# Routing of the last tiles and the closing stage rearranged in a decoder layer on one Trainium2 core

## What is computed

```python
        out = mix @ w_out[l]
        x = x + gate_m * rmsnorm(out, g_post_mix[l])

        h = rmsnorm(x, g_pre_ffn[l]) * (1.0 + scale_f) + shift_f
        y = hier_moe(h, w_router_g[l], b_router_g[l], w_router_e[l], b_router_e[l],
                     w_e_gate[l], w_e_up[l], w_e_down[l])
        x = x + gate_f * rmsnorm(y, g_post_ffn[l])
```

## Time and profile before

| | us |
|---|---|
| median of 3 runs | 769.46 |
| lowest and highest | 768.12 to 769.5 |
| the profiled execution | 773.03 |
| its span, first to last instruction | 771.4 |
| PE busy | 688.9 (89%) |
| VectorE (DVE) busy | 413.4 (54%) |
| ScalarE (ACT) busy | 291.5 (38%) |
| GpSimd (POOL) busy | 119.1 (15%) |
| moved by DMA | 179.27 MB, mean 232 GB/s |

### The profile page before, as it was taken

The page is one execution under the profiler, slowest core; times in us unless marked ns, Lnnn a source line. Parts: engine busy times, 40 slices in busy tenths (PEclk is TensorE's granted clock), DMA queues, the critical chain, the costliest instruction groups (busy, mean ns, idle before and its releaser), DMA issues.

```text
span 771.4 us, 9644 instructions
## 1 busy us (share of the span) xinstructions
PE 688.9 (89%) x3419; PEld 436.3 (57%) x3419; DVE 413.4 (54%) x876; ACT 291.5 (38%) x526; POOL 119.1 (15%) x143
## 2 busy tenths in 40 slices
PE   1899989999998989999999999989799979788873
PEld 0447757666676767777787788764333323233321
DVE  2376967998888877554423836645342211211118
ACT  5141336454586659442224333442221211211223
POOL 3056772320001101000000001010122211111100
...
GB/s 338 380 295 402 253 207 1 119 96 15 110 54 56 2 110 1 68 42 110 110 154 157 28 381 100 326 411 391 423 419 420 419 419 420 420 420 412 407 295 109
DMA packets 50270, 179.27 MB, mean 232 GB/s; under 512 B 9593, under 2 KB 13796, under 8 KB 36398
## 3 DMA queue, kind: packets, MB, share of 16 engines
...
...
## 4 chain that ended last, share of the span: by engine, by line
PE 43%; DVE 22%; DMA 7%; issue 7%; SPq 5%; ACT 4%; DVEq 0%; POOL 0%; ACTq 0%; POOLq 0%
PE psA L485 8%; PE psA L487 7%; PE psA L486 7%; PE psS L898 6%; PE psA L927 5%; SPq L1105 4%; DVE mk_mem L1856 4%; PE psG L898 4%; DVE m L1855 3%; DMA arena<-in_w_e_up_dram 3%; DVE arena_r L1804 2%; DMA y_dram<-sig_mem,tables 2%; DVE mk_mem L1895 1%; DVE qs_mem L1875 1%; DVE qs_mem L2023 1%
## 5 line engine op out<-in xcount | busy, mean ns | idle before, releaser
L485 PE MATMUL psA<-arena_r 128*128 128x512 f32 x320 | 129.6, 405 | 0.6 <-PE psA L487 0.6
L487 PE MATMUL psA<-arena_r 128*128 128x512 f32 x320 | 125.4, 392 | 0.0
L486 PE MATMUL psA<-arena_r 128*128 128x512 f32 x320 | 125.2, 391 | 0.0
L1804 DVE TENSOR_TENSOR arena_r<-arena,arena_r 128x1024 fp32r<-128x1024 f32 (+1 forms) x37 | 61.5, 1686 | 32.2 <-ACT arena_r L1322 31.1
L898 PE MATMUL psS<-arena,kv 128*64 128x512 f32 x224 | 62.9, 646 | 12.1 <-issue 9.7
L485 PEld LDWEIGHTS psA<-arena_r 128*128 128x128 f32 x320 | 60.7, 190 | 21.3 <-issue 9.5
L487 PEld LDWEIGHTS psA<-arena_r 128*128 128x128 f32 x320 | 60.4, 189 | 13.2
L486 PEld LDWEIGHTS psA<-arena_r 128*128 128x128 f32 x320 | 60.7, 190 | 11.8 <-issue 0.2
L898 PE MATMUL psG<-arena,kv 128*64 128x512 f32 x208 | 58.2, 611 | 5.0 <-issue 5.0
L1322 ACT CAST arena_r<-arena 128x1024 fp32r<-128x1024 f32 (+1 forms) x34 | 49.9, 1499 | 15.6 <-DMA arena<-in_w_in_dram 10.0
L2314 DVE TENSOR_TENSOR sig_mem<-sig_mem,psS 128x256 f32<-128x256 f32 x8 | 4.9, 613 | 81.1 <-ACT sig_mem L1642 81.1
...
## 6 DMA issues: line engine op xcount, KB each, us to landing
...
```

The source lines that it names most:

```text
L485: nc.tensor.matmul(acc, lhs[0], rhs[0], start=start, stop=False)
L486: nc.tensor.matmul(acc, lhs[0], rhs[1], start=False, stop=False)
L487: return nc.tensor.matmul(acc, lhs[1], rhs[0], start=False, stop=stop)
L1804: V.tensor_tensor(lo[:, part], src[:, part], hi[:, part], ALU.subtract).then_inc(lo_ready, 4 if q is None else 1)
```

## The change

At the routing of the last tiles: the squares of tile 3 are summed in halves with the copies of its transposes between; tile 2's rows are scaled and stored after tile 3's root; GpSimd makes the members, first_hot of tile 2 and the pair columns of tiles 2 and 3; PE runs slots(0), slots(1) and half of first_rows(0) ahead of tile 3's transposes, which go to banks S0 and A0; ranks(2) and position(2) come before route(3) on VectorE. The product of gates moves from there to after the gather of pair 1, its copy to pair 1. The third set of weights is issued in two parts, gate weights after k = 3 of the last output half, up weights at its end. In the closing stage all tiles go through the banks in order, and VectorE weighs tiles 0 and 1. At the layer's start one semaphore that nobody waits for is replaced by VectorE's own. The core of the diff:

```diff
         hi_n, lo_n = cnt[:, 5, 0:2 * TT], cnt[:, 6, 0:2 * TT]
         rowid = sb("rowid", [P, 2, TT, 2])
-        diag_e = kv[:, 1024:2048]
...
+                    if (tt, n, k) == (TT - 1, 1, 3):
+                        last.then_inc(ring_out, 1)
                 last.then_inc(full, 1)
-                if (tt, n) == (TT - 1, 1):
-                    pe.wait_ge(full, bank[where[("out", tt, 1)]].at[("out", tt, 1)] + 1)
-                    pe.sem_inc(ring_out, 1)
...
             def slots(tt):
...
-                pe.wait_ge(pos_ready, tt + 1)
+                if tt < 2:
+                    pe.wait_ge(pos_ready, tt + 1)
+                else:
+                    pe.wait_ge(pool_choice, columns[tt])
+                    if tt == 3:
+                        pe.wait_ge(pos_ready, 3)
+                    else:
+                        pe.wait_ge(dve_choice, lo2)
...
-            def first_rows(tt):
-
-                pe.wait_ge(hot_ready, tt + 1)
-                for half in range(2):
+            def first_rows(tt, halves=(0, 1)):
+
+                if tt == 2:
+                    pe.wait_ge(pool_choice, hot2)
+                else:
+                    pe.wait_ge(hot_ready, min(tt, 2) + 1)
+                for half in halves:
...
             router(2)
-            pe.wait_ge(spread_rows, 2)
-            gate_rows(diag_e, "gf", ("A0",))
-            x1_turn(3)
-            g = take("A1", ("gf", 1))
-            nc.tensor.matmul(g[:, :], ones[:, :], diag_e[:, 512:1024], start=True, stop=True).then_inc(bank["A1"].full, 1)
-            router(3)
             slots(0)
             slots(1)
-            first_rows(0)
+            first_rows(0, (0,))
+            x1_turn(3, ("S0", "A0"))
+            router(3)
+            ranks(2)
+            first_rows(0, (1,))
             first_rows(1)
-            ranks(2)
+            first_rows(2, (0,))
             ranks(3)
+            first_rows(2, (1,))
             slots(2)
-            first_rows(2)
             slots(3)
             first_rows(3)
+            gf_turn = [bank[f"A{n}"].turn(("gf", n)) for n in range(2)]
...
+            def ffn_gate_rows():
+
+                pe.wait_ge(spread_rows, 2)
+                for n in range(2):
+                    pe.wait_ge(bank[f"A{n}"].free, gf_turn[n])
+                    nc.tensor.matmul(ps[f"A{n}"][:, :], ones[:, :], diag_e[:, n * 512:(n + 1) * 512], start=True, stop=True).then_inc(bank[f"A{n}"].full, 1)
...
                 if j < NPAIR - 1:
                     turn_rows(j + 1, (j + 1) % 2, j // 2)
+                if j == 0:
+                    ffn_gate_rows()
...
-                    last = nc.tensor.matmul(ps[name][:, :], last_hot[:, tt, :], yb[:, 1, 512 * half:512 * (half + 1)], start=True, stop=(tt == 0))
-                if tt == 0:
-                    last.then_inc(sum_full, 1)
+                    nc.tensor.matmul(ps[name][:, :], last_hot[:, tt, :], yb[:, 1, 512 * half:512 * (half + 1)], start=True, stop=False)
...
             pe.wait_ge(yb_ready, NPAIR)
-            for tt in range(3):
+            for tt in range(TT):
                 last_part(tt)
-            other_part(1)
-            last_part(3)
-            other_part(2)
-            other_part(3)
+                other_part(tt)
...
+            def third_gate_up(n):
+                for q in range(2):
+                    src = (weg_v, weu_v)[n]
+                    sp.dma_start(gu_sets[2][q][:, 2048 * n:2048 * (n + 1)], src[4 + q]).then_inc(we_in[2], 16)
+
             sp.wait_ge(ring_out, len(items))
-            gate_up(2, 0, 4)
-            gate_up(2, 1, 5)
+            third_gate_up(0)
             down(1, 0, 2)
+            filled(sp, ("out", TT - 1, 1))
+            third_gate_up(1)
             down(1, 1, 3)
             sp.wait_ge(x1_ready, 2 * TT)
-            sp.wait_ge(xss_ready, TT)
+            sp.wait_ge(xss_ready, TT + 1)
...
-            pool.tensor_tensor(diag_e.rearrange("p (k n) -> p k n", k=KD), ident[:, :].unsqueeze(1).broadcast_to([P, KD, P]),
-                               gatev[:, 1, :].unsqueeze(2).broadcast_to([P, KD, P]), ALU.mult).then_inc(spread_rows, 1)
+            def members(tt):
+
+                pool.wait_ge(dve_choice, signed[tt])
+                step(pool.tensor_tensor(first_in[:, tt, :], e12[:, :, tt, 0], e12[:, :, tt, 1], ALU.subtract))
+                pool.tensor_tensor(first_in[:, tt, :], first_in[:, tt, :], st[:, 60 + tt:61 + tt].broadcast_to([P, 2]), ALU.mult).then_inc(pool_choice, 1)
...
+            def pair_columns(tt):
+
+                odd = e12[:, :, tt, :].rearrange("p w (n a) -> p w n a", a=2)
+                step(pool.tensor_tensor(pool_pair, odd[:, :, :, 0], odd[:, :, :, 1], ALU.subtract))
+                for w in range(2):
+                    ins = pool.tensor_tensor(hi_hot[:, tt, w, :, :], pool_pair[:, w, :].unsqueeze(1).broadcast_to([P, 2, NPAIR]),
+                                             rowid[:, w, tt, :].unsqueeze(2).broadcast_to([P, 2, NPAIR]), ALU.mult)
+                    if w == 0:
+                        step(ins)
+                    else:
+                        ins.then_inc(pool_choice, 1)
+                pool.wait_ge(pool_choice, columns[tt])
...
+            members(2)
+            pool.wait_ge(dve_choice, lo2)
+            step(pool.tensor_tensor(first_hot[:, 2, :], lo_hot[2][:, 0, :], first_in[:, 2, 0:1].broadcast_to([P, P]), ALU.mult))
+            step(pool.tensor_tensor(causal0[:, :], lo_hot[2][:, 1, :], first_in[:, 2, 1:2].broadcast_to([P, P]), ALU.mult))
+            pool.tensor_tensor(first_hot[:, 2, :], first_hot[:, 2, :], causal0[:, :], ALU.add).then_inc(pool_choice, 1)
+            pool.wait_ge(pool_choice, hot2)
+            pair_columns(2)
+            members(3)
+            pair_columns(3)
...
                     gather(src_i[:, j:j + 1], j % 2)
+                if j == 1:
+                    pool.tensor_tensor(diag_e.rearrange("p (k n) -> p k n", k=KD), ident[:, :].unsqueeze(1).broadcast_to([P, KD, P]),
+                                       gatev[:, 1, :].unsqueeze(2).broadcast_to([P, KD, P]), ALU.mult).then_inc(spread_rows, 1)
...
+            def last_half_squares(half):
+
+                act.wait_ge(x1_ready, 2 * TT - 1 + half)
+                nc.scalar.activation(scratch[:, 512 * half:512 * (half + 1)], x1(TT - 1)[:, 512 * half:512 * (half + 1)], ACT.Square,
+                                     accum_out=m8[:, 0:1] if half else st[:, 33:34]).then_inc(xss_ready, 1)
+
+            last_half_squares(0)
+            turned(3)
+            last_half_squares(1)
+            x1_root(3)
             store_rows(2)
-            x1_part(3)
             store_rows(3)
...
-                if j == 0:
+                if j == 1:
                     gate_copy()
...
-                if tt == 0:
-                    act.wait_ge(sum_ready, 1)
-                    nc.scalar.activation(scratch2, yc[:, tt, 0, :], ACT.Square, accum_out=st[:, tt:tt + 1]).then_inc(fms_ready, 1)
-                    return
...
             nc.scalar.activation(st[:, 44:45], st[:, 34:35], ACT.Sqrt)
-            first_choice(0)
-            first_choice(1)
-            square(0)
-            first_choice(2)
-            rooted(0)
-            first_choice(3)
-            for tt in range(1, TT):
+            for tt in range(TT):
                 square(tt)
+                if tt < 2:
+                    first_choice(tt + 2)
                 rooted(tt)
...
+            def mean_x1(tt):
                 dve.wait_ge(xss_ready, tt + 1)
+                if tt == TT - 1:
+                    dve.wait_ge(xss_ready, tt + 2)
+                    step(V.tensor_tensor(st[:, 33:34], st[:, 33:34], m8[:, 0:1], ALU.add))
                 rsqrt_in(st[:, 34:35], st[:, 33:34], D).then_inc(xms_ready, 1)
+
+            def scale_x1(tt):
                 dve.wait_ge(xsq_ready, tt + 1)
                 step(V.reciprocal(st[:, 60 + tt:61 + tt], st[:, 35:36]))
                 dve.sem_inc(xr_ready, 1)
 
+            def root_x1(tt):
+                mean_x1(tt)
+                scale_x1(tt)
...
-                dve.wait_ge(pos_ready, tt + 1)
+                dve.wait_ge(pos_ready, min(tt, 2) + 1)
+                if tt == TT - 1:
+                    dve.wait_ge(pool_choice, taken[3])
...
+                if tt >= 2:
+                    if tt == 2:
+                        mean_x1(3)
+                    V.tensor_tensor(e12[:, :, tt, :], e12[:, :, tt, :], sgn.unsqueeze(1).broadcast_to([P, 2, NE]), ALU.mult).then_inc(dve_choice, 1)
+                    dve.wait_ge(dve_choice, signed[tt])
+                    return
...
             route(2)
-            root_x1(3)
+            position(2)
+            scale_x1(3)
             route(3)
-            first_member(2)
-            first_member(3)
-            position(2)
-            first_slots(2)
             position(3)
             first_slots(3)
...
-                dve.wait_ge(fw_ready, tt + 1)
+                if tt < 2:
```

(41 more changed lines are left out.)

31 lines of the change are left out of this document (21 added, 10 removed).

## The result

| | before | after |
|---|---|---|
| median of 16 runs | 768.31 | 771.86 |
| lowest and highest | 765.71 to 770.73 | 770.13 to 773.91 |
| the profiled execution | 773.03 | 770.62 |
| its span | 771.4 | 769.1 |

The account below looks back on a forecast made before the run. The weights' DMA stream was taken to bound the kernel up to about 733 us, VectorE the tail; 1.2 us from stream holes plus 2.0 from the tail, 3.2 off the median 769.46, made 766.3 us, range 764.2 to 769.6.

Parts of the forecast that it names:

- product 0's end at 517.2: First expert pair's gate and up product: ends 2.4 us sooner, at 517.2 instead of 519.57; the set behind it issued then.
- the gather goes at 516.0: Gather of pair 1's rows on GpSimd: issued at 516.0, 2.9 us later than 513.07.
- I take 3.0: Time pair 1's gather takes: 3.0 us, between bounds of 2.6 (idle queue) and 7.82 (full queue), landing at 519.0.
- The queue ran dry: DMA queue ahead of the set behind product 0: all queued weights end near 517 us.
- the start of tile 3's routing: Tile 3's routing on VectorE: starts 0.4 us later than 502.26, waiting for position(2) and ranks(2).
- the squares in halves: Tile 3's squares in halves: copies come forward only by what the work put ahead of them takes, so no gain.
- The last store: Row stores on ScalarE: last issued at 506.0, not 504.13, queued behind the other, landing near 515.1.
- Product 1: Pair 1's gate and up product: runs 7.09 us as before, ending at 529.1 against 529.28.
- The stream: Expert weights' DMA stream: holes sum to 2.3 us instead of 3.5, so 1.2 us less.
- The third set's 2.07: Third weight set, issued at about 491 instead of 494.61: its stream hole of 2.07 us closes.
- The tail: Closing stage on VectorE: ends at 766.5 instead of 768.74, taken as 2.0 us less, between 1.0 and 3.0.
- The rival: Pair 1's gather takes 6.5 us, TensorE's clock halves, product 1 ends at 535.5: +4.0 us, 773.5; chance 0.14.

Follow-up runs that it names:

- e13: Changed kernel, SP issuing the fourth weight set only after a small GpSimd fill behind the issue of pair 1's gather: 765.75 us, 0.9966 of the kernel before.
- e3: Changed kernel with one more SP wait, the fourth weight set issued only when pair 1's gather has landed: 768.23 us, 0.9980 of the kernel before.
- e14: Changed kernel, SP issuing the fourth weight set only when GpSimd has made the diagonal of gates: 767.86 us, 0.9981 of the kernel before.
- e4: Changed kernel with the scaling and store of tile 2's rows back ahead of tile 3's squares: 764.69 us, 0.9941 of the kernel before.
- e9: Changed kernel with 23 filler products on TensorE in its wait for pair 1's rows: 770.50 us, 1.0022 of the kernel before.
- e8: Changed kernel with the third weight set issued only after the last output half, as before: 771.88 us, 1.0047 of the kernel before.
- e11: e1 with the third weight set issued early: 766.03 us, 0.9960 of the kernel before.
- e1: Kernel before with the new closing stage alone: 765.69 us, 0.9947 of the kernel before.

## Why the prediction was wrong

**The step that failed is product 0's end at 517.2 (+54.5), with what was hung on it: "the gather goes at 516.0", 1.2 us ahead of the set behind product 0, and "I take 3.0".** The gather went at +53.38 where +53.3 was forecast, and with a lead its price is nearly right, as far as the runs show (none has the 1.2 us itself): e13, with 1.38 us of lead, has 3.55 us and is 0.9966 of before, 2.6 us of gain where 3.2 were forecast. But product 0 ended at +52.90, 1.6 us before its forecast, and so the weights were issued 0.44 us ahead of the gather instead of 1.2 behind it. The gather took 9.65 us. I priced it by how full the queue would be, between 2.6 and 7.82 us, and the 9.65 lie outside that range. I never asked which of the two issues comes first, though both times stood in the text. The queue ran dry at about +53.4 where +54.3 was forecast, so it was not what made the gather late: in e3, e13 and e14 it was as quick as hoped. A step that came out better than forecast turned the sign.

Of the 1.6 us, 1.1 are the start of tile 3's routing, which I put 0.4 later. It came 0.7 sooner: 496.63, which is +38.88, against 502.26 or +39.58.

```profile
496.63 0.22 DVE L2219 SCALAR_TENSOR_TENSOR gp<-psG,st,rowb 128x4 f32<-128x4 f32 x1
```

I had let "nothing" come of the squares in halves and had left out that the scaling of tile 2's rows, 2.1 us on ScalarE, no longer stands ahead of them. e4, which puts it back, starts this routing at 498.02 (+39.72) and ends product 0 later, 0.84 us each; the other 0.3 us no run takes apart. From there VectorE needs 4.9 us to the end of first_hot (501.5, +43.8; forecast 5.0, +45.0), and GpSimd's pair columns release PE at 501.29, after a wait of 0.64, beside VectorE as forecast.

**The last store.** Issued at +42.19, not +43.3, it is followed by the gather 11.2 us later. I had 10.0 (9.1 and 0.9), two stores one behind the other. That it started 1.1 us sooner and took 1.2 longer cancelled in the gather's issue, so the forecast of +53.3 was right by luck.

**Product 1.** Forecast "as before", at +66.4; it ended 8.1 us behind that. Of it 6.65 are the gather's 9.65 instead of 3.0, and 1.4 the transposes and gate products, which took 4.39 us at half clock where I had 3.0 at full; e9 has 2.74.

**The stream.** I forecast holes of 2.3 us for 3.5. The third set's 2.07 was the first term and came to next to nothing: in e8 and e11 the hole closed ahead of a late issue only moves. In all runs in which product 1 ends at +67.5 or later, e14 alone left out, product 15 ends 208.0 to 208.7 us after it, whether the third set is early or late; where it ends sooner, 209.5 to 210.9 us after it. This fits a stream that is set by the fifth set's issue, which hangs on product 1, where I had summed holes; but e14, with 210.9, does not fit, and no run moves that issue alone.

**The tail** was right in size: 2.5 us by the mark, 3.3 in the medians of e1, for 2.0 (1.0 to 3.0). VectorE begins 5.4 us behind product 15's end (forecast 5.5) and has one gap of 0.81 us and two of 0.27, for 0.4 each:

```profile
745.82 0.75 DVE L2438 TENSOR_SCALAR arena<-arena,rtmp_mem 128x1024 f32<-128x1024 f32 x1 [0.72 <-DVE sig_mem L2398]
...
750.68 1.42 DVE L2448 TENSOR_TENSOR arena<-psT,gla_mem 128x512 f32<-128x512 f32 x2 [0.81 <-ACT qs_mem L1768]
...
765.00 1.41 DVE L2460 SCALAR_TENSOR_TENSOR qT<-arena,st,qT 128x512 f32<-128x512 f32 x2
```

**The rival.** "The gather is late and TensorE's clock falls: slower, 773.5" is what happened, at 0.14, though for another reason than the full queue that it named. It had the clock at half speed, product 1's end at 535.5 (+72.8; it was +74.5) and 4.0 us of loss; 3.6 were measured, and so near only by luck, as the gather took 9.65 us where the rival had 6.5. It was given too little because its condition was put as a gather of 5.5 us in a queue "near its end", and not as an order of two issues 1.2 us apart, in a text whose own terms for either of them were good to 1 or 2 us.
